# Three passes of rounded parts for the projections of three attention mixers

## The reference, cut to what matters

```python
# MLA: h = modulated rms norm of x; w_in 1024 x 672
lat = h @ mla_w_in;  ...;  x += gate * (heads @ mla_w_out)
# mixer_ab
p = jnp.einsum('bsd,de->bse', x, w_in)          # 1024 x 3584 and 8 gates
ya = dilated_attention(aq, ak, av, rel_bias)     # 8 heads of 64
yb = jax.nn.sigmoid(bo) * head_norm(mlstm(bq, bk, bv, bi, bf), head_g)
return jnp.einsum('bse,ed->bsd', jnp.concatenate([ya, yb], -1), w_out)
# mixer_c: w_in 1024 x 2560 and 24 gates, three branches of attention, w_out
```

## Time and profile before

| | |
|---|---|
| median of 3 runs | 2677.16 us (2674.88 to 2678.27) |
| the profiled execution | 2677.69 us, its span 2675.9 us |
| mean granted TensorE clock | 0.976 |
| instructions in the span | 36507 |
| weights and other data read | 496.33 MB, 187 GB/s over the span |

### The profile page before, as it was taken

How to read it: one execution, slowest core, us unless ns; L and a number is a source line. 1 busy time by engine, 2 the same in 40 slices (tenths; PEclk the granted TensorE clock), 3 DMA queues, 4 the chain that set the end, 5 groups by cost and what they waited for, 6 DMA issues and landing times.

```text
span 2675.9 us, 36507 instructions
## 1 busy us (share of the span) xinstructions
PE 2543.9 (95%) x15410; PEld 2211.9 (83%) x15410; DVE 1607.2 (60%) x2236; ACT 1000.9 (37%) x1237; POOL 81.5 (3%) x116
## 2 busy tenths in 40 slices
PE   4999999999999999999999999999999988999998
PEld 3999758999999778897999677788887857788886
DVE  5986155876886455543755333547984144647985
ACT  2333034334333032222433122536772132446773
POOL 0000000000000003440000000000000000000000
PEclk9999989999999998999999998999999999999999
DMA  6886302774876230001644610647994320647991
GB/s 286 330 317 225 118 24 91 303 287 152 308 292 239 97 116 24 1 1 56 241 175 160 181 65 1 275 180 307 369 351 176 144 84 1 252 189 289 373 371 51
DMA packets 48266, 501.82 MB, mean 188 GB/s; under 512 B 4968, under 2 KB 9448, under 8 KB 10856
## 3 DMA queue, kind: packets, MB, share of 16 engines
q1 hardware_dynamic: 42480, 490.52, 48.4%
q10 hardware_dynamic: 5624, 8.97, 1.3%
HBM read 496.33 MB, written 3.15 MB: 187 GB/s over the span
## 4 chain that ended last, share of the span: by engine, by line
PE 83%; DVE 9%; DMA 4%; ACT 2%; issue 1%; POOL 1%; ACTq 0%; DVEq 0%; POOLq 0%
PE PS L511 25%; PE PS L1074 24%; PE PS L557 12%; PE PS L475 2%; DMA bias_scratch<-work 2%; PE PS L819 2%; PE PS L832 2%; PE PS L828 1%; DMA ring<-stream 1%; PE PS L910 1%; PE PS L1171 1%; PE PS L468 1%; PE PS L494 1%; DVE work L1660 1%; DMA xT<-x_in 1%
## 5 line engine op out<-in xcount | busy, mean ns | idle before, releaser
L511 PE MATMUL PS<-x_part_hi,w_up_hi 128*128 128x256 f32 x1408 | 404.5, 287 | 9.9 <-DVE x_part_lo L1717 6.5
L511 PE MATMUL PS<-x_part_hi,w_up_lo 128*128 128x256 f32 x1408 | 399.5, 284 | 0.0
L511 PE MATMUL PS<-x_part_lo,w_up_hi 128*128 128x256 f32 x1408 | 399.4, 284 | 0.0
L2212 DVE TENSOR_TENSOR ring_low<-ring,m_w_up 128x2048 fp32r<-128x2048 f32 x128 | 293.1, 2291 | 133.9 <-ACT m_w_up L1518 133.9
L1518 ACT ACTIVATE m_w_up<-ring 128x2048 fp32r<-128x2048 f32 x128 | 245.2, 1916 | 187.1 <-PE PS L1074 187.0
L511 PEld LDWEIGHTS PS<-x_part_hi,w_up_hi 128*128 128x128 f32 x1408 | 271.2, 193 | 13.2 <-issue 8.0
L511 PEld LDWEIGHTS PS<-x_part_lo,w_up_hi 128*128 128x128 f32 x1408 | 271.4, 193 | 0.0
L511 PEld LDWEIGHTS PS<-x_part_hi,w_up_lo 128*128 128x128 f32 x1408 | 271.1, 193 | 0.0
L1074 PE MATMUL PS<-m_w_up,xg_hi 128*128 128x512 f32 x640 | 253.0, 395 | 3.8 <-DVE work L2226 3.8
L1074 PE MATMUL PS<-ring_low,xg_hi 128*128 128x512 f32 x640 | 254.1, 397 | 0.0
L1074 PE MATMUL PS<-m_w_up,xg_lo 128*128 128x512 f32 x640 | 253.2, 396 | 0.0
(11 more groups left out here) (451 smaller groups left out, 4493.6 us busy)
## 6 DMA issues: line engine op xcount, KB each, us to landing
ring<-stream SPq DMA_DIRECT2D x133, 2048.0 KB, 7.8
ring<-stream SPq DMA_DIRECT2D x88, 1536.0 KB, 6.6
work<-stream SPq DMA_DIRECT2D x48, 1024.0 KB, 7.7
hT<-stream SPq DMA_DIRECT2D x16, 1024.0 KB, 7.4
ring<-stream SPq DMA_DIRECT2D x3, 1152.0 KB, 5.7
const<-const_tables ACTq DMA_DIRECT2D x1, 2336.5 KB, 18.3
bias_scratch<-work ACTq DMA_DIRECT2D x1, 2048.0 KB
work<-bias_scratch ACTq DMA_DIRECT2D x2, 1024.0 KB, 8.9
```

Source lines behind the costliest of these rows:

```text
L511: last = mm(out, w[a][:, lo:lo + P], x[b][:, at:at + T], start=start and i == 0, stop=stop and i == 2, skip_group_check=skip)
L2212: tt_(ring_low[n][:, part], ring[n][:, part], m_w_up[g % 3][:, :].bitcast(F32), ALU.subtract).then_inc(S("up_split"), 1)
```

## The change

Every input and output projection of mla, ab and c (not the gates) is done as in the ffn phases: three passes of rounded parts. A weight piece is cut into two halves of 256 columns (mla_in.1: 128 and 96). For each half ScalarE writes the high part to one of three buffers (`mix_high`; from the fourth on it waits until TensorE has used the half three before, `mh_used`), VectorE writes the remainder over the piece in the ring (`mix_lows`), and TensorE waits for it (`low_done`). The pieces are then freed by `mh_used`, the end of their second half. In ab and c the input itself is split: ScalarE copies it a quarter at a time (`x_high`), VectorE takes the remainders (`x_lows`); mla uses the ffn way (`shifted_high`, `shifted_low`). The heads' outputs are rounded by ScalarE out of PSUM, and VectorE takes the remainder and signals `att_out`. The output projection's first half starts tile by tile as heads are ready, and the residual or layer norm follows each half. The first two halves of mla and ab are made at the end of ffn0 and ffn3, those of c at the end of moe0. The order of the other work is kept, with the new steps set between. The diff, cut; `...` marks what is left out.

```diff
+SPLIT = [name for name, _ in STREAM if name.startswith(("mla_in", "mla_out", "ab_in", "ab_out", "c_in", "c_out"))]
...
+        half_high = [rounded("half_high0", 20992, 2048), rounded("half_high1", 23040, 2048), down_low_ring[3]]
...
+            if name in SPLIT:
+                return S("mh_used"), HALF_AT[name] + 2
...
+            TERMS = ((0, 0), (0, 1), (1, 0))
+            def half_tiles(g, x, mtiles, rows=P, ks=range(KT), passes=None):
+                pe.wait_ge(*low_done(g))
...
+                            for a, b in terms:
...
+                                last = mm(bank(m // 2, T, (m % 2) * T, 0, rows), w[a][:, k, j * step:(j + 1) * step],
+                                          x[b][:, k * T:(k + 1) * T], start=first[j] and (passes is None or j == 0),
+                                          stop=stop, skip_group_check=passes is not None)
...
+                last.then_inc(S("mh_used"), 1)
...
+            def out_split(ph, ks, ready):
                 for i in range(2):
-                    take(f"{tag}.{i}")
-                    project(f"{tag}.{i}", i, src, range(4 * i, 4 * i + 4))
+                    split_piece(f"{ph}_out.{i}", mix_y[ph], range(4 * i, 4 * i + 4), ks,
+                                None if i else [(ready, TERMS)])
...
                 norm_sums()
-                hold(6, 14)
-                line.next("h_ready")
-                take("mla_in.0")
-                project("mla_in.0", 0, h3, range(0, 4))
...
+                hold(6, 7)
+                split_piece("mla_in.0", x_parts, range(0, 4), passes=[(lambda k: line.next("x_split"), TERMS)])
...
-                pe.wait_ge(S("att_out"), 16)
-                out_proj("mla_out", tiles(W(M_O, U)))
+                out_split("mla", range(KT), lambda k: pe.wait_ge(S("att_out"), 2 * k + 2))
...
-                take("ab_in.6")
                 pe.wait_ge(S("ab_copied"), 1)
-                project("ab_in.6", 6, x3, range(0, 4))
+                split_piece("ab_in.6", mix_x, range(0, 4))
...
-                pe.wait_ge(S("stab_ready"), 1)
-                project("ab_in.0", 0, x3, range(12, 16))
+                pe.wait_ge(S("rowbc_read"), 1)
+                split_piece("ab_in.0", mix_x, range(12, 16))
...
+            def mix_high(g):
...
+                if g - PHASE_AT[ph] >= 3:
+                    act.wait_ge(S("mh_used"), g - 2)
+                fn(high_of(g), half_of(g), ACT.Copy).then_inc(S("mh_high"), 1)
+            def x_high(ph):
+                for b in range(4):
+                    act.wait_ge(S("x_ready"), XR[ph] - 3 + b)
+                    part = slice(512 * b, 512 * (b + 1))
+                    fn(mix_x[0][:, part], xT[:, part], ACT.Copy).then_inc(S("mx_high"), 1)
...
-                    line.done(fn(o, bank(4 + it["h"] % 2, T, 0, lo, lo + dv), ACT.Copy), "att_out")
+                    fn(y_parts(phase, it)[0], bank(4 + it["h"] % 2, T, 0, lo, lo + dv),
+                       ACT.Copy).then_inc(S("x_rounded"), 1)
...
-                attention("mla")
+                attention("mla", {i: [lambda i=i: mix_highs("mla", i // 2 + 2)] for i in (4, 6, 8)})
...
             def ab():
+                mix_highs("ab", 2)
+                x_high("ab")
                 line.next("bias_ready")
...
+                mix_highs("ab", 3)
                 copied_raw(3, 0)
+                mix_highs("ab", 4)
                 act.wait_ge(slot_free, FREED["ab_gates"])
...
                 act.wait_ge(S("bias_stored"), 16)
                 load_bias(A_BM)
+                mix_highs("ab", 5)
                 copied_raw(4, 2)
+                mix_highs("ab", 6, 7)
                 copied(5, W(A_BV, 1024), 4)
+                mix_highs("ab", 8)
                 line.next("conv_ready")
                 fn(W(A_BQ, 2048), W(A_BQ, 2048), ACT.Silu).then_inc(S("bqk_ready"), 1)
+                mix_highs("ab", 9)
...
                 fn(ls(4352, 1024), flat(4, 2), ACT.Copy).then_inc(S("lnum_copied"), 1)
...
+                mix_highs("ab", 15)
+                line.next("lin_moved")
+                fn(ls(5376, 1024), ls(4352, 1024), ACT.Square).then_inc(S("lin_rooted"), 1)
...
+                attention("ab", {2: [lambda: mix_highs("ab", 16)], 5: [linear_high]})
+                mix_highs("ab", 17)
...
+            def mix_lows(ph, *steps):
+                for i in steps:
+                    g = PHASE_AT[ph] + i
+                    dve.wait_ge(S("mh_high"), g + 1)
+                    tt_(half_of(g, True), half_of(g), high_of(g).bitcast(F32), ALU.subtract).then_inc(S("mh_split"), 1)
...
+                def output_low(i):
...
+                    tt_(low, bank(4 + it["h"] % 2, T, 0, lo, lo + dv), hi.bitcast(F32),
+                        ALU.subtract).then_inc(S("att_out"), 1)
-                for step in range(n + 2):
+                for step in range(n + ATT_DEEP + 1):
                     if step < n:
                         maxima(step)
-                    if step >= 2:
+                    if 2 <= step < n + 2:
                         normalise(step - 2)
...
+                    if step >= 5:
+                        output_low(step - 5)
...
+                attention("mla", {i: [lambda i=i: mix_lows("mla", (i + 1) // 2 + 1)] for i in (5, 7, 9)})
...
+                x_lows()
+                mix_lows("ab", 2, 3)
                 done(v.memset(raw[:, :, 0:3], 0.0))
...
                 dve.wait_ge(S("ab_copied"), 1)
+                mix_lows("ab", 4, 5)
                 conv(0, 4)
...
                 dve.wait_ge(S("ab_copied"), 2)
+                mix_lows("ab", 6, 7)
                 conv(4, 8)
+                mix_lows("ab", 8, 9)
                 line.next("rowbc_ready")
...
+                mix_lows("ab", 10, 11, 12, 13)
...
+                mix_lows("ab", 14)
+                attention("ab", {0: [lambda: mix_lows("ab", 15)], 4: [linear_out, lambda: mix_lows("ab", 16)], 6: [linear_low]})
+                mix_lows("ab", 17)
+                layer_norm("ab", 0, by_half("ab"))
...
+                x_lows()
+                mix_lows("c", 2, 3, 4, 5, 6, 7, 8)
                 dve.wait_ge(S("c_copied"), 3)
...
+                attention("c", {i: [lambda i=i: mix_lows("c", (i - 1) // 3 + 8)] for i in (7, 10, 13)})
```

276 lines of the change are left out of this document (191 added, 85 removed).

## The result

The changed kernel takes 2688.07 us (median; 2679.34 to 2697.05) where the kernel before, on the same chips, takes 2675.36 (2670.86 to 2682.51). The ratio is 1.0042, 95% interval [1.0033, 1.0052]: 11.2 us slower. The profiled execution's span is 2685.9 us, 10.0 above that of before.

The account below looks back on a forecast made before the run. TensorE was busy 95% of the span, but costs were read stage by stage, with `ab`'s queues behind the bias store deciding. MLA -1.3, `ab` +20.5 and `c` -6.7 gave +12.5 us, so 2690; range 2683 to 2697, with rivals 2676 to 2704.

Parts of the forecast that it names:

- MLA, -1.3 forecast: MLA stage: input -5.5 us, attention +10.2 from VectorE's added remainders, output -6.0; together -1.3 us.
- The chain in `ab`: `ab`: rounding half 5 waits for the bias store; 28.2 us in series after it where 4.8 stood, ab_in.6 26.1 late.
- cold start: `ab`, ab_in.5: TensorE runs mostly at 1.2 GHz after its long stop, costing 2 us, bounds 1 and 4.
- The four pieces: `ab` input after ab_in.5: four pieces gain 2.3 us each, plus 0.6 of old slow start: -9.8 us.
- The attention of `ab`: `ab` attention: VectorE is busy 16.75 of 18.5 us, so all its added work counts: +8.0 us, bounds 6.3 and 9.2.
- `ab` together: Whole `ab` stage: VectorE arrives 18.2 us late, attention +8.0, output and its end -5.7; sum +20.5 us.
- `c`, -6.7 forecast: `c` stage: input -11.0 us, attention +10.0 from VectorE's remainders, output -5.7; together -6.7 us.
- The price of a pass: Changed projections: a rounded pass of 256 columns costs 120.7 ns on TensorE, three 362 ns against 433 to 436.
- rival 4: Projections: passes come at the columns' pace, 20 us less over 560 products, giving 2670 us; chance 0.03.
- the attentions absorb the work: Three attention loops: VectorE's idle time takes its new work, at most 13.8 us; not slower if all absorbed; chance 0.13.
- the falling clock: Attentions: remainders idle TensorE nine times and its clock falls, 1.5 us each, up to +13, 2704 us; chance 0.08.
- a shorter store: `ab`: the bias store ends sooner; 26 us shorter, `ab` loses nothing and the whole takes 2664 us; chance 0.04.

Follow-up runs that it names:

- a3: The changed kernel with 26 idle products added on TensorE in the `ab` attention; ratio 1.0058 to the kernel before.
- a4: The changed kernel with the nine weight remainders inside the three attentions cut to four columns; ratio 0.9982 to the kernel before.
- b1: a4 with the remainders of the attentions' outputs cut to four columns too; ratio 0.9962 to the kernel before.
- b2: The changed kernel with `ab` work moved before the store waits, gates before remainder 5, store issued after the input's first quarter; ratio 0.9945 to the kernel before.

## Why the prediction was right

Forecast +12.5 us and 2690; measured +11.2 and 2688.1. The mechanism was right in the stage that decides, not only the sum: the stop in `ab` stood where three queues read together had put it, and held TensorE for 33.5 us, 37 forecast. By its terms:

- **MLA, -1.3 forecast, -4.1 measured** (with ffn0's tail, +1.1 of 1.15). Input: forecast -5.5; the products after the latents' norm start 4.9 us sooner (306.9, 302.0), and 1.7 more were gained up to the first maxima, which no term had. Attention: forecast +10.2 (5.8 to 12.6), measured +7.5, the term that was mis-sized. I had set it near the upper bound; VectorE's idle time took up more, and fell from 10.5 to 5.7 us. A part of the miss may be scatter: a3, with the same code there, had 50.2 us, +9.6.
- **The chain in `ab`.** ab_in.6, counted from the start of the norm sums, is 24.6 us late; forecast 26.1, of which 1.1 are ffn3's tail and outside this count, so 25.0. ab_in.5 took 13.17 us: with 11.4 for a warm piece the cold start is 1.8, 2 forecast.
- **The four pieces, -9.8 forecast.** ab_in.0, 1 and 2 start 21.4, 19.0 and 16.5 us late, the attention's first maxima 15.9; forecast for VectorE's arrival 18.2, less the tail 17.1.
- **The attention of `ab`, +8.0 forecast, +8.3 measured; of `c`, +10.0 and +10.1.** With a4 and b1 the cause is shown for the most part, not only the size: 17.5 of the 25.8 us of all three went with the weights' remainders.
- **`ab` together, +20.5 forecast with the tail, +18.8 without it measured.**
- **`c`, -6.7 forecast, -8.6 measured.** Attention and output (5.7 less, both) as forecast; the input gained 12.9 us up to the compression in place of 11.0.
- **The price of a pass.** Forecast 120.7 ns, from the ffn rows. `c`'s output took 22.21 us over 192, 115.7 ns; `ab`'s 116.7; MLA's 119.4; warm pieces in `ab` 118.3, and `c`'s first 312 passes 119.2. So the outputs' 5.0 to 5.7 us, counted from their first product, came from shorter passes; an earlier start would show in the length of the attentions, and no run tells it apart there. A part of rival 4 was true: nearly half way to 109 ns in `c`'s output.

The rivals. **1**, the attentions absorb the work: they grew by 25.8 us, 28.2 forecast; refuted. **2**, the falling clock: it fell, in `ab` for 27 us on end, but the three attentions together grew by 2.4 us less than the forecast, which had no such term, so its +13 did not come on top. It isn't free: 0.5 us in `ab` between 0.72 and 0.56, and 4 us in `c` in the two kernels with 0.74, 2.8 of them in the tail. **3**, a shorter store: 49.5 us; refuted. **4**, passes at the columns' 109 ns: none came under 115.7.

That the sum came out within 1.3 us is luck in part: MLA and `c` gained 2.8 and 1.9 us more than forecast, and the last stretch and the middle lost 1.9 and 1.8, which is their scatter.

## What to carry to other kernels

When an operation is split so that engine A prepares for B and B for C, read each in-order queue for the waits ahead of the new instruction: one 1.9 us rounding placed behind a wait for a DMA cost 17 us, and moving that one line gave it back. In a software-pipelined loop over several engines, look at an item's round through them before work is moved: VectorE's sum priced what was added to it well (+8.3 and +10.1 us for 8.0 and 10.0), but moving work to an idler engine gained nothing where it added a hop, and small blocks spread over the items cost less than whole ones in `ab` and `c`, and in MLA up to its tail. Read a stop from the engine's own timeline, not from the chain of waits, before a gain is promised from it. And after a wait is removed, ask at once what ends last next; a part of b2's 9 us went that way.

## What was not expected of the hardware

- The clock granted to TensorE stayed at 0.50 for 27 us in an attention in which TensorE was busy 27.3 of 30.8 us, and with the clock at 0.72 in the mean the same attention took only 0.5 us less. In the tail of `c`'s attention, where TensorE is busy without a gap, the same products took 4.23 us at 1.00 and 6.99 at 0.53.
- While GpSimd ran a 128x2048 subtraction from SBUF (4.5 us), VectorE's multiplications by a scalar took up to 4.39 us and ended just after it, even one of 128x8 elements (3.80 us in place of 0.17); its reductions and the maxima, which read PSUM, did not.
- Rounded passes of 256 columns came at 115.7 ns in `c`'s output, where the DMA engines were busy 1% of the time, and at 119.4 in MLA's, where they were busy a quarter of it; no run tells whether that is the reason.
- The same 2 MB store took 49.4 to 49.8 us in twelve kernels and 52.6 and 52.9 in the two that issued it between ScalarE's roundings of the input. The cause is open.
